# First attention of a two-block transformer: queries and keys by columns of the weights, memory's norm after them

## What is computed

```python
def _mixer_ab(h, w_in, q_norm, w_uq, kv_norm, w_ukv, sinks, w_out, cos, sin):
    proj = jnp.einsum('bsd,df->bsf', h, w_in)                 # 1440 columns
    c_q, c_kv, k_r, q_s, k_s, v_s = _split_cols(proj, AB_SPLITS)   # 384, 256, 32, 512, 128, 128
    q = jnp.einsum('bsr,rf->bsf', _rms_norm(c_q, q_norm), w_uq)
    kv = jnp.einsum('bsr,rf->bsf', _rms_norm(c_kv, kv_norm), w_ukv)
    ...
    o_a = _mla_attention(...)                                 # 8 heads, from q and kv
    o_b = _swa_sink_attention(q_s, k_s, v_s, sinks)           # 8 query heads, 2 key heads
    return jnp.einsum('bsf,fd->bsd', concat(o_a, o_b), w_out)

def _swa_sink_attention(q, k, v, sinks):
    alibi = -_alibi_slopes(SWA_HEADS) * jnp.abs(dist)         # slope 2 ** -(h + 1) for head h
    logits = jnp.einsum('bcqkgd,bcskd->bckgqs', qc, kb) * d ** -0.5 + alibi
    p = softmax(concat([where(valid, logits, NEG_INF), sink]))[..., :-1]
    return jnp.einsum('bckgqs,bcskd->bcqkgd', p, vb)
...
mem_n = rms_norm(mem, mem_norm_g)                             # second block
```

## Time and profile of the kernel before

| | |
|---|---|
| three timed runs | 923.22, 923.25, 923.54 us (median 923.25) |
| the profiled execution | 923.38 us |
| its span in the trace | 921.3 us |
| granted TensorE clock, mean | 0.999 of full speed |
| HBM read | 167.49 MB, 183 GB/s over the span |

### The profile page before, as it was taken

One profiled execution on the slowest core, in us unless ns is written; L12 is line 12 of the kernel. 1 busy time (PEld: TensorE's weight loads), 2 busy tenths in 40 slices (PEclk: granted clock), 3 DMA queues, 4 the chain that ended last, 5 costly groups with the idle time before them and its releaser, 6 DMA issues.

```text
span 921.3 us, 12786 instructions
## 1 busy us (share of the span) xinstructions
PE 909.3 (99%) x4754; PEld 762.9 (83%) x4754; DVE 608.1 (66%) x1000; ACT 507.7 (55%) x816; POOL 37.6 (4%) x53
## 2 busy tenths in 40 slices
PE   8999999999999999999999999999999999999997
PEld 7888878888888898877888888887888888888875
DVE  4888687666663767768766666376656587574665
ACT  4785564655552456666465555255557664555434
POOL 1100034000000001000000000001000000000000
PEclk9999999999999999999999999999999999999999
DMA  8654467755574668443755556454564465555651
GB/s 317 253 182 137 136 196 207 253 193 190 191 246 124 136 186 259 131 164 147 267 183 188 192 191 237 131 182 145 192 206 130 157 203 163 165 157 181 205 172 57
DMA packets 72556, 169.39 MB, mean 184 GB/s; under 512 B 11304, under 2 KB 33216, under 8 KB 71856
## 3 DMA queue, kind: packets, MB, share of 16 engines
q1 hardware_dynamic: 69680, 156.10, 52.1%
q0 software_dynamic: 2816, 12.48, 4.2%
HBM read 167.49 MB, written 1.06 MB: 183 GB/s over the span
## 4 chain that ended last, share of the span: by engine, by line
PE 93%; DVE 2%; DMA 2%; ACT 2%; issue 0%; SPq 0%; DVEq 0%; POOL 0%; ACTq 0%
PE psum L734 21%; PE psum L902 14%; PE psum L906 7%; PE psum L683 7%; PE psum L685 7%; PE psum L688 7%; PE psum L935 7%; PE psum L940 3%; PE psum L826 3%; PE psum L836 3%; PE psum L830 3%; PE psum L1037 2%; PE psum L1068 1%; DMA arena<-in_mem 1%; PE psum L1051 1%; PE psum L655 1%
## 5 line engine op out<-in xcount | busy, mean ns | idle before, releaser
L1593 DVE TENSOR_TENSOR base_lo<-stage,base_hi 128x1024 fp32r<-128x1024 f32 (+3 forms) x222 | 262.1, 1204 | 96.6 <-ACT base_hi L1220 95.6
L1220 ACT CAST base_hi<-stage 128x1024 fp32r<-128x1024 f32 (+3 forms) x222 | 223.9, 1035 | 53.0 <-PE psum L688 24.3
L1593 DVE TENSOR_TENSOR extra_lo<-stage,extra_hi 128x1024 fp32r<-128x1024 f32 (+1 forms) x68 | 80.0, 1201 | 48.3 <-ACT extra_hi L1220 47.9
L683 PE MATMUL psum<-base_hi,xt 128*128 128x512 f32 (+2 forms) x272 | 107.1, 394 | 0.8 <-ACT xt L1255 0.3
L685 PE MATMUL psum<-base_lo,xt 128*128 128x512 f32 (+2 forms) x272 | 104.7, 385 | 1.7 <-DVE base_lo L1593 1.4
L688 PE MATMUL psum<-base_hi,xt 128*128 128x512 f32 (+2 forms) x272 | 104.6, 385 | 0.0
L1220 ACT CAST extra_hi<-stage 128x1024 fp32r<-128x1024 f32 (+1 forms) x68 | 68.1, 1030 | 50.2 <-PE psum L734 32.3
L902 PE MATMUL psum<-xt,extra_hi 128*128 128x512 f32 x320 | 87.3, 394 | 0.0
L734 PE MATMUL psum<-base_hi,ht 128*128 128x512 f32 x288 | 87.3, 393 | 0.0
L935 PE MATMUL psum<-xt,base_hi 128*128 128x512 f32 x240 | 76.5, 403 | 0.0
L902 PE MATMUL psum<-xt,base_hi 128*128 128x512 f32 x256 | 69.7, 394 | 0.0
(11 more groups left out here) (233 smaller groups left out, 1543.4 us busy)
## 6 DMA issues: line engine op xcount, KB each, us to landing
stage<-in_w_up SPq DMA_DIRECT2D x80, 512.0 KB, 4.5
stage<-in_w_down SPq DMA_DIRECT2D x44, 512.0 KB, 4.4
stage<-in_w_in_a SPq DMA_DIRECT2D x22, 512.0 KB, 4.7
stage<-in_w_cd_in SPq DMA_DIRECT2D x16, 512.0 KB, 4.9
stage<-in_w_in_b SPq DMA_DIRECT2D x12, 512.0 KB, 3.6
stage<-in_w_ab_in SPq DMA_DIRECT2D x11, 480.0 KB, 6.4
ln_par<-in_ln POOLq DMA_DIRECT2D x4, 1024.0 KB, 6.8
stage<-in_w_ab_out SPq DMA_DIRECT2D x8, 512.0 KB, 3.6
```

The source lines that it names most:

```text
L683: pe.matmul(acc, ah, wh, start=(k == 0), stop=False)
L1220: act.copy(w_hi(c, 0, w), stage_of(c, w)).then_inc(hi_done, 1)
L1593: dve.tensor_tensor(w_lo(c, 0, w), stage_of(c, w), w_hi(c, 0, w).bitcast(F32), ALU.subtract).then_inc(lo_done, 1)
```

## The change

**The SWA heads' queries and keys are made transposed.** "ab_in" keeps the two low ranks, the rope key and the two value heads: 800 columns by token, 2 steps of 400 (chunks n = 0 to 7). The second step's chunks are loaded in three pieces each (272, 64 and 64 columns). A new product "ab_qk" follows, 8 chunks of one input block and 640 columns each, loaded in two pieces (keys, 2 groups of 64; queries, 2 groups of 256). In it the weights are the held operand, five blocks of 128 columns (block 0: both keys; blocks 1 to 4: the queries of heads p and p+4), summed at once in PSUM banks 0 to 4, input chunk by input chunk; a block is one matmul of 512 (tokens high and low, L1179) and one of 256 (low weights, L1184). The last two chunks go block by block. The sums lie transposed, so no pair of 0 to 3 is transposed or copied by `turn_pair` and `copy_pair`, and `copy_key` goes. ScalarE copies the low half of each sum out (`copy_swa_lows`), VectorE adds the high half (`add_swa_lows`), first for blocks 0 and 1, then for 2 to 4. A pair is now heads p and p+4, so the first four chunks of the output product's weights are loaded as two halves each.

**The distance table.** Only head 0's 384 columns are loaded; GpSimd multiplies them by 2 ** -h for the other seven heads.

**Order.** The query rank's norm stands behind chunk 5 of "ab_in", memory's behind 6, the value rank's behind 7, each but the last with the due splits ahead of it. The query rank is transposed at n=7 of "ab_in"; the value rank behind chunk 2 of "ab_qk", memory behind its chunks 3 and 5; the copy and the addition of the first low sums, and the load of ScalarE's table for exponentials, behind 6; pair 0's logits behind 7. Other banks serve for the transposes (`TURN_BANKS`).

```diff
-    table = [("ab_in", 8, 2, 480, 3), ("uq", 3, 3, 256, 3), ...
+    table = [("ab_in", 8, 2, AB_TOKEN // 2, 2), ("ab_qk", 8, 1, SWA_W, 1), ("uq", 3, 3, 256, 3), ...
...
-L0_PLACES = ([("ab_in", 10), ("ab_in", 11)] + [("uq", n) for n in range(3)] + ...
+L0_PLACES = ([("ab_qk", 6), ("ab_qk", 7)] + [("uq", n) for n in range(3)] + ...
...
-            load("swa", table, d["swa"])
+            load("swa", table[:, 0, :], d["swa"][:, 0, :])
             load("rope", rope[:, :, :, :], d["rope"])
+            pool.wait_ge(loaded["swa"], 16)
+            for h in range(1, SWA_H):
+                pool.tensor_scalar(table[:, h, :], table[:, 0, :], 2.0 ** (-8 * h // SWA_H), None, ALU.mult
+                                   ).then_inc(table_made, 1)
...
+                for k in range(g.kc - 2):
+                    for b in (0, 1, 4, 2, 3):
+                        if (k, b) == (0, 4):
+                            pe.wait_ge(turn_lo, turned_at("x0", 1, 7))
+                        if (k, b) == (0, 2):
+                            pe.wait_ge(acc_free[(g.u0 + 1) % 2], 2 * ((g.u0 + 1) // 2))
+                        last = block(k, b)
+                    last.then_inc(chunk_used, 1)
+                    if k in between:
+                        between[k]()
+                for b in range(5):
+                    for k in (g.kc - 2, g.kc - 1):
+                        last = block(k, b)
+                        if b == 4:
+                            last.then_inc(chunk_used, 1)
+                    if b == 1:
+                        last.then_inc(first_blocks, 1)
+                between[g.kc - 1]()
...
             gemm("ab_in", xt_hi, xt_lo, 0, "x0",
-                 {7: lambda: turn("mem", tile_of(mem_x), [(rms_done, 1)], [0]),
-                  8: lambda: turn("mem", tile_of(mem_x), [(rms_done, 2)], [1]), 
-                  9: turn_queries,
-                  10: lambda: [heads_banks("cq"), attend("ab_in", 10),
-                               turn("ckv", tile_of(proj0, Q_RANK), [(rms_done, 6)])],
-                  **attending("ab_in", 11)},
+                 {7: turn_queries},
                  second=turn_tokens)
-            pe.wait_ge(turn_lo, turned_at("ckv", 1, 1))
+            queries_and_keys({2: turn_ranks, 3: lambda: turn("mem", tile_of(mem_x), [(rms_done, 3)], [0]),
+                              5: lambda: turn("mem", tile_of(mem_x), [(rms_done, 4)], [1]),
+                              **attending("ab_qk", 7)})
...
+            beyond = PRODUCTS["ab_qk"].c0 + NS
+            gemm("ab_in", copy_to(lambda j, t, acc: (proj0[:, t, j * FIRST:(j + 1) * FIRST], acc[:, 0:FIRST])),
+                 {5: lambda: [split_to(done["due"]), query_rank_norm()], 6: lambda: [split_to(done["due"]), memory_norm()],
+                  7: lambda: [split_to(beyond), turn("cq", ht_hi, 8), value_rank_norm()]})
+            gemm("ab_qk", None, {2: lambda: turn("ckv", ht_hi, 11), 3: lambda: turn("mem", ht_hi, 0, [0]),
+                                 5: lambda: turn("mem", ht_hi, 0, [1]),
+                                 6: lambda: [copy_swa_lows(0), act.preload_act_table(ACT.Exp)], 7: first_pair})
...
+            def add_swa_lows(n):
+                u, dst, highs, lows = swa_sums(n)
+                dve.wait_ge(block_lows, n + 1)
+                dve.tensor_tensor(dst, dst, highs, ALU.add).then_inc(acc_free[u % 2], TT)
...
+            def first_pair():
+                add_swa_lows(1)
                 dve.wait_ge(loaded["swa"], 16)
+                dve.wait_ge(table_made, SWA_H - 1)
                 dve.wait_ge(loaded["heads"], 16)
-                attend("ab_in", 10)
+                attend("ab_qk", 7)
```

229 lines of the change are left out of this document (138 added, 91 removed).

## The result

The changed kernel takes 925.02 us (median of 15 runs, 923.82 to 925.98), the kernel before 923.25 on the same chips: a ratio of 1.0016, 95% interval 1.0009 to 1.0023. So it is slower, by 1.5 us by the ratio; the two medians are 1.8 us apart. The forecast was 921.9, its range 919.4 to 924.6.

What follows compares the result with a forecast made beforehand. TensorE, busy 99% of the span, was taken to bound the kernel: 923.38 - 0.8 (pair 0's probabilities turned earlier) - 0.7 (pairs 2 and 3 no longer turned) = 921.9 us, range 919.4 to 924.6.

Steps and rivals of the forecast that it cites:

- no wait but 0.05 us on the way to the first logits: Up to the first logits, terms sum to -1.9 us: logits near 44.9 instead of 46.77 us.
- value rank's norm: Norm needed after the third block chunk, called the key rank's: it just fits, 0.05 us taken, at worst 1.
- The pieces: Weight chunks loaded in several pieces: splits have four chunks of lead, some 7 us, so no cost was taken.
- rival B: Chance 0.16: weights in pieces or the key rank's norm come late, some 1.5 us before the first logits; 923.4 us.
- the due splits ahead of both norms: Changed queue order in the token projection: the wait for a low part at 29.7 us goes, 0.9 us gained.
- Masking 2.5 us behind the logits: Pair 0's masking, queued behind the last three blocks' addition, begins 2.5 us after the logits, at 47.4 instead of 47.75 us.
- the turning 8.2 us behind that: TensorE turns pair 0's probabilities 8.2 us after masking begins, at 55.6 instead of 56.38 us: -0.8 us.
- a wait for the maxima: Before turning pair 0's probabilities, TensorE, ready at about 53.5 us, waits about 2 us, replacing three short waits.
- The later pairs: Pairs 2 and 3 are no longer turned: 2 x 0.35 us, so -0.7 us; VectorE keeps up.
- Rival D: Chance 0.09: the removed turns stood in slack, VectorE's copies set the pace, only the 0.8 us remain; 922.6 us.
- C: Rival, chance 0.12: GpSimd's seven multiplications keep VectorE out, 1.2 us lost to each; the end comes near 928 us.
- The rule of the Trainium skill: VectorE and GpSimd share an exclusive port lock per instruction; each split beside a multiplication would wait for all of it.

Runs made afterwards that it cites:

- e1: The changed kernel with each chunk of the token projection's second step loaded in one piece instead of three; 924.08 us, ratio to before 1.0011.
- e2: As e1, with each chunk of the queries' and keys' product also one load instead of two; 923.60 us, ratio to before 1.0004.
- e3: The kernel before with chunks 4 to 7 of its first product loaded in three pieces each; 924.98 us (one run).
- e6: The changed kernel with the query rank's norm ahead of the due splits and memory's norm behind the value rank's; 927.49 us, ratio to before 1.0036.
- e7: e2 and e6 together, with ScalarE's exponentials table loaded ahead of memory's second transposes; 925.13 us, ratio to before 1.0017.
- e9: e7 with the value rank's casts and low parts ahead of memory's second norm, and pair 0's masking ahead of the last addition; 922.16 us, ratio 0.9992.
- e8: The changed kernel with the whole distance table loaded and GpSimd's seven multiplications left out; 927.98 us, ratio to before 1.0048.
- e4: The changed kernel with VectorE's addition of blocks 2 to 4 behind the masking of pair 0; 924.57 us, ratio to before 1.0008.
- e10: e9 with GpSimd's loads of memory and its gain issued later, behind the small ones; 925.00 us, ratio to before 1.0021.
- e12: e9 with GpSimd's loads of masks, norm parameters and wsp waiting longer; 921.89 us, ratio to before 0.9987.

## Why the prediction was wrong, point by point

**What bounds the kernel, and the projections' cost: right.** In after a matmul of 400 columns starts 0.182 us behind the last (0.455 ns a column), a pair of 512 and 256 columns 0.350 us (0.456 ns).

**The step that failed is "no wait but 0.05 us on the way to the first logits".** Its sum was -1.9 us, the trace has +0.30 (47.07 against 46.77). Term by term, as excess of a start-to-start distance over the engine's own pace (the first row as it says):

| term | forecast | measured |
|---|---|---|
| first pass (second pass starts 1.25 us earlier, of which 0.88 is width) | -0.1 | -0.4 |
| wait for a low part at 29.7 us | -0.9 | -0.9 |
| key copies (42.23 to 43.16 us before) | -0.6 | -0.7 |
| pair 0's transposes | -0.35 | -0.35 |
| value rank's norm | +0.05 | +0.54 |
| weights landing late, 22.98 to 24.80 us | 0 | +1.46 |
| evacuation behind memory's norm, 30.67 to 31.19 us | 0 | +0.40 |

They add to +0.05; the other 0.25 us is spread over the stretch. Two terms had been put at nothing. The pieces: the forecast named them, had no row for them, and left them to rival B with "four chunks of lead, some 7 us"; the landing took 10.9 us from issue, since three pieces each stood between parts of GpSimd's loads, the later ones issued behind them (e1, e2, e3). The order: the forecast counted "the due splits ahead of both norms" as a gain alone. It is also a wait added to the norms, and it was not asked what is queued behind the waiting split. That split wants a chunk that TensorE needs 5 us later, and holds the query rank's norm, memory's norm, the evacuation and the value rank's norm behind it until the chunk lands (24.57 us in after; 2.35 us of waiting in e1). The queue from the evacuation to the last norm was sized rightly, 5.8 us forecast and 5.7 measured (30.27 to 35.96), but it began 1.2 us after TensorE had gone on to the transposes (29.09), where before a like queue had begun 0.2 us after (32.42 and 32.22), and the forecast had set both off together. With the order alone changed both waits are gone (e6; also e7 and e9). That edit moved the splits and memory's norm at once, so how much each of the two orders cost is not shown.

**Masking 2.5 us behind the logits, the turning 8.2 us behind that, a wait for the maxima: right** (2.52, 8.24, 1.39 us; the wait is 0.6 shorter than the 2 us forecast, since TensorE itself came later by the evacuation at 54.03 us, 0.69). As the chain is fixed from the logits on, the 2.2 us missed ahead of them went straight to the end: 55.6 + 2.2 = 57.8, against 57.83. The select ran at 49.59 us beside masks that read PSUM and cost nothing, as hoped.

**The later pairs: -0.7 forecast, -0.4 measured** (from the turning of pair 0's probabilities to that of pair 3's: 57.83 to 84.08 us in after, 56.38 to 83.04 before). Rival D had a part: with pair 3's transposes gone TensorE waits 0.59 us for ScalarE's copy of the probabilities at 70.07.

**The rivals.** B was the case. It said 923.4; with its 1.5 us at the 2.2 that it took, and -0.4 for the later pairs, it gives 923.4 + 0.7 + 0.3 = 924.4. The span grew by the same 1.1 us; the profiled 924.1 is 0.3 less because 1.7 us lay around the span instead of 2.1. One of its conditions held, a norm more than 0.3 us late; the other only in kind, since the late low part was a token chunk's and not a block chunk's. C is refuted: 0.09 us lost to each split in the mean, at most 0.35, not 1.2, and the load avoided is worth 3 us (e8). The rule of the Trainium skill (SBUF — State Buffer, section Who interferes with whom) would have had each split wait for a whole multiplication; here a split of 640 elements took between 0.81 and 1.17 us beside multiplications of 1.2 to 2.0, and 0.82 without, so for the multiplications the trace doesn't agree. It does for a lock held over a whole instruction at the select (e4, 50.21 us), which two small instructions waited out; but these have one input tensor, so they aren't the form with two SBUF inputs that the prediction took the rule for.

**The range** ended at 924.6, below the median, because B's landing was given 1.5 us and nothing for what changes from run to run: two traces of after differ by 0.9 us.

**One reading of the prediction was off and cost nothing.** It calls the two waits of 0.7 us the longest of TensorE's. The longest is one of 1.1 us for `qk_t` at 1.12 us, at the start of the program, and it is the same in both kernels.

What stays open: what in the chip lets the same load land up to a microsecond sooner or later from run to run, whether e9's remaining wait of 0.73 us ahead of memory's transposes can be had without another bank, which wasn't tried; and what the repairs would give in the kernel before. The landings in A and B aren't all that differs from run to run: there is the wait at 317.7 us in e4 and e10, and a kernel's longer runs often have a lower mean granted clock of TensorE. Of e12's twelve runs the three above 924 us had 0.995 and 0.996, the nine others, up to 922.66 us, 0.998 and 0.999. What lowers it is not shown.

## What to carry to other kernels

Before a split that is due is put ahead of other work, ask when its data lands and what stands behind it on that engine: a wait for a DMA holds everything queued there, and a chunk that the matmul engine wants 5 us later can hold a norm that it wants sooner. Lay weights out so that a chunk is one load, above all where another queue loads beside it, and look which loads it is issued behind; and when an engine gets faster, look at what it issues next and what that will meet. A chain is often two links wide: moving the addition or the table load alone took 0.25 and 0.4 us off B, with the rest of the order repaired B fell by 1.4 us.

## What the runs showed of the hardware

- The same bytes land later in three pieces: 480 KB took 6.4 us from issue in one piece and 11.9 us in three (e3, issued 12.67 and landed 24.52 us), beside 1.9 MB from GpSimd's queue. Part of it is the later issue of the last pieces. And the two queues moved like numbers of packets, not of bytes: 267 packets with 1.04 MB beside 269 with 0.11 MB between 16 and 19 us of after.
- VectorE's small instructions stopped for GpSimd's select, which runs from SBUF to SBUF: two of 128x2 elements took 0.98 us beside it at 50.17 us (e4), 0.36 without it, and four scalings 1.54 instead of 1.01. Masks that read PSUM took their usual 0.28 and 0.42 us beside the select at 49.59 us of after.
- GpSimd lost more than VectorE where its multiplications met VectorE's work: one of 384 elements took 1.16 us alone (e9, 27.79 us) and up to 2.00 beside VectorE, seven took 11.18 us in after and 8.64 in e9.
